# Searching key tiles 2 to 6 in the first part of a streaming encoder layer, with sixteen of twenty-six rounds on ScalarE

## What is computed

```python
h = rmsnorm(x, g_pre)
u_a, gate_a, q, k, v, qi, ki, wi, gate_b = split(h @ w_in)
# index scores: 8 heads of width 32
dots  = einsum('bqhd,bkd->bqhk', qi, ki)
score = einsum('bqh,bqhk->bqk', wi, relu(dots)) * INDEX_SCALE
score = where(key_chunk <= query_chunk, score, -inf)     # chunks of 64
_, sel = top_k(score, 256)
# softmax attention of 8 query heads over the selected keys only, with a bias by distance,
# times silu(gate_b); the pool branch times silu(gate_a); concat -> w_out -> rmsnorm -> + x
```

## Time and profile before

| | |
|---|---|
| runs (median of 3) | 1626.82 us (1625.3 to 1630.24) |
| the profiled execution | 1626.64 us, its span 1624.8 us |
| TensorE busy | 1494.8 us (92%) |
| VectorE busy | 1141.5 us (70%) |
| ScalarE busy | 889.3 us (55%) |
| GpSimd busy | 455.9 us (28%) |
| granted TensorE clock, mean | 0.98 |

### The profile page before, as it was taken

The page is one execution under the profiler, slowest core; times in us unless marked ns, Lnnn a source line. Parts: engine busy times, 40 slices in busy tenths (PEclk is TensorE's granted clock), DMA queues, the critical chain, the costliest instruction groups (busy, mean ns, idle before and its releaser), DMA issues.

```text
span 1624.8 us, 17105 instructions
## 1 busy us (share of the span) xinstructions
PE 1494.8 (92%) x4935; PEld 841.4 (52%) x4935; DVE 1141.5 (70%) x2742; ACT 889.3 (55%) x1684; POOL 455.9 (28%) x387
## 2 busy tenths in 40 slices
PE   7999899989999999988788888989998989899996
PEld 4555555555554887756334444444444444455552
DVE  5412577769899566765388898999999889874412
ACT  3112333333334445553898888988997877533331
POOL 0111211121110322311444444344423333232341
PEclk9999999999999999988899999999999999999999
DMA  9322222231111211136822222331130211203011
GB/s 368 68 60 47 78 55 64 56 102 48 60 50 51 67 42 37 49 113 181 240 60 90 84 74 57 96 99 61 43 105 27 70 39 45 72 16 105 33 40 45
DMA packets 93158, 125.69 MB, mean 77 GB/s; under 512 B 17309, under 2 KB 64221, under 8 KB 92682
## 3 DMA queue, kind: packets, MB, share of 16 engines
q1 hardware_dynamic: 91834, 120.68, 23.8%
q10 hardware_dynamic: 1232, 3.93, 2.2%
HBM read 75.93 MB, written 47.61 MB: 76 GB/s over the span
## 4 chain that ended last, share of the span: by engine, by line
PE 25%; DVE 15%; issue 7%; ACT 5%; DMA 0%; POOL 0%; POOLq 0%; DVEq 0%; SPq 0%; ACTq 0%
PE wide L1791 9%; PE wide L1776 8%; DVE above L345 5%; DVE max_junk L1852 4%; PE bank L1751 2%; PE bank L1752 2%; PE bank L1753 2%; ACT act_junk L1667 2%; PE bank L1724 2%; DVE above L377 1%; ACT E L1704 1%; PE wide L1724 1%; DVE root L296 1%; ACT sq L1689 1%; DVE reach L378 1%
## 5 line engine op out<-in xcount | busy, mean ns | idle before, releaser
L938 PE MATMUL bank<-hT,home 128*128 128x512 f32 (+2 forms) x1280 | 485.9, 515 | 5.1 <-DVE sga L1153 2.4
L1627 POOL TENSOR_TENSOR E<-E,home 128x512 f32<-128x512 f32 (+1 forms) x174 | 226.5, 1305 | 460.0 <-ACT E L1704 460.0
L938 PEld LDWEIGHTS bank<-hT,home 128*128 128x128 f32 x1280 | 235.1, 191 | 164.6 <-issue 143.3
L1776 PE MATMUL wide<-E,home 128*128 128x512 f32 x544 | 281.9, 600 | 0.7 <-POOL E L1627 0.7
L1704 ACT ACTIVATE E<-bank 128x512 f32<-128x512 f32 (+1 forms) x290 | 165.4, 570 | 206.1 <-PE bank L1753 186.9
L914 ACT ACTIVATE relu<-wide 128x1024 f32<-128x1024 f32 (+7 forms) x192 | 154.0, 802 | 214.3 <-PE wide L956 154.2
L1192 DVE SCALAR_TENSOR_TENSOR S<-relu,wi,S 128x1024 f32<-128x1024 f32 (+7 forms) x168 | 173.8, 1035 | 101.6 <-ACT relu L914 94.2
L1852 DVE CUSTOM_DVE_ANT_0 max_junk<-bank,mask 128x512 bf16<-128x512 f32 (+3 forms) x235 | 138.3, 606 | 85.4 <-PE bank L1724 71.9
L1791 PE MATMUL wide<-home 128*128 128x512 f32 x272 | 140.9, 609 | 26.3 <-ACT osb L1693 26.0
L1667 ACT ACTIVATE act_junk<-S,minus_cand 128x1152 uint8<-128x1152 f32 (+5 forms) x105 | 155.5, 1481 | 1.6
L956 PE MATMUL wide<-kiT,qiT 96*128 96x512 f32 (+3 forms) x304 | 137.9, 522 | 7.2 <-ACT relu L914 7.2
(11 more groups left out here) (215 smaller groups left out, 2225.5 us busy)
## 6 DMA issues: line engine op xcount, KB each, us to landing
xs<-x_prompt SPq DMA_DIRECT2D x16, 512.0 KB, 4.2
home<-w_in SPq DMA_DIRECT2D x16, 512.0 KB, 13.2
xr<-x_prompt SPq DMA_DIRECT2D x16, 512.0 KB, 4.1
y_prompt<-osb SPq DMA_DIRECT2D x16, 512.0 KB, 2.8
first_q<-q_high_scratch SPq DMA_DIRECT2D x24, 256.0 KB, 4.6
s_scratch<-S SPq DMA_DIRECT2D x11, 512.0 KB, 2.7
gb<-gb_scratch SPq DMA_DIRECT2D x17, 256.0 KB, 4.9
home<-ma_scratch SPq DMA_DIRECT2D x17, 256.0 KB, 5.0
```

Source lines behind the costliest of these rows:

```text
L938: mm = pe.matmul(out, stationary(c), moving(c), start=(c == 0), stop=(c == DC - 1))
L1627: pool.tensor_tensor(E[:, k % 4, :, 0:n], E[:, k % 4, :, 0:n], EB[:, kv * GRP:(kv + 1) * GRP, off:off + n], ALU.mult)\
L1776: pe.matmul(wide[0][:, kv * 512:kv * 512 + GRP * n].rearrange("p (j n) -> p j n", j=GRP), values[:, kt, kv:kv + 2, :].rearrange("p a d -> ...
```

## The change

Tile 6 joins `EARLY`, and `FIRST` becomes 7. An early tile's search is now one scaling pass on ScalarE (SN), sixteen single rounds on ScalarE (SK), ten single rounds on VectorE (SP) and the four parts of the choice one by one (SC). `seek` is called by `project`: it takes portions until their planned costs pass the room (3.4 us a projection, 1.87 in the blocks of two and three tiles, 3.4 for every TM), and lays them evenly between the pieces of the projection. A load or a store of the search is placed only where no portion is taken. ScalarE's scratch row changes its type to 8 bits. VectorE gets one more wait on its own chain before it overwrites unseen scores. The code that builds the second part's order is the same and works on ten tiles instead of eleven.

```diff
+SEARCH_ROOM = 3.4
...
-EARLY = range(TOPK // P, 6)
-SEARCH_PIECES = [(r, min(r + 4, ALL_ROUNDS)) for r in range(0, ALL_ROUNDS, 4)]
+EARLY = range(TOPK // P, 7)
+CHOICES = 4
...
+def early_search(t):
+    n = key_tiles(t)
+    return ([(("SN", t), 0.14 * n)] + [(("SK", t, r), 0.143 * n + 0.78) for r in range(ZOOM_AT)]
+            + [(("SP", t, r), 0.155 * n + 0.45) for r in range(ZOOM_AT, ALL_ROUNDS)]
+            + [(("SC", t, part), 0.3 * n + 0.3) for part in range(CHOICES)])
...
-    def project(step, left):
+    def project(step, left, room=0.0):
         k = -(-len(pending) // left) if left > 0 else 0
         pieces = [pending.pop(0) for _ in range(min(k, len(pending), 2 * DC if step[0] == "TM" else DC))]
         aside = [short.pop(0) for _ in range(min(len(short), 2))]
         for i, piece in enumerate(aside):
             pieces.insert((i + 1) * (len(pieces) + len(aside) - i) // (len(aside) + 1) if pieces else i, piece)
         inside[step] = pieces
-        steps.extend(pieces)
+        seek(list(pieces), room)
         steps.append(step)
 
-    def seek():
-
-        if seeking:
-            steps.append(seeking.pop(0))
-            if steps[-1][0] == "SM" and seeking:
-                steps.append(seeking.pop(0))
+    def seek(pieces, room):
+
+        taken = []
+        while seeking and room > 0 and seeking[0][0][0] not in ("SL", "SM"):
+            item, cost = seeking.pop(0)
+            taken.append(item)
+            room -= cost
+        if not taken:
+            while seeking and seeking[0][0][0] in ("SL", "SM"):
+                steps.append(seeking.pop(0)[0])
+        marks = sorted([((i + 0.5) / len(pieces), 0, x) for i, x in enumerate(pieces)]
+                       + [((i + 0.4) / len(taken), 1, x) for i, x in enumerate(taken)], key=lambda m: m[:2])
+        steps.extend(x for *_, x in marks)
...
+            room = (SEARCH_ROOM if nt == 4 else 0.55 * SEARCH_ROOM)
             if t:
-                seek()
-                project(("TM", t), 1 + sum(taking))
+                project(("TM", t), 1 + sum(taking), SEARCH_ROOM)
                 pool_part()
             cached = 0 <= t - 4 < PAST // P
             for j, step in enumerate(mine):
                 scale(2)
-                if step[0] != "Q":
-                    seek()
-                project(step, sum(taking[j:]) if taking[j] else 0)
+                project(step, sum(taking[j:]) if taking[j] else 0, room)
...
             if t - 1 in EARLY:
-                seeking.append(("SL", t - 1))
-                seeking += [("SP", t - 1, *piece) for piece in SEARCH_PIECES]
-                seeking.append(("SM", t - 1))
-                if len(seeking) == len(SEARCH_PIECES) + 2:
-                    steps.append(seeking.pop(0))
+                seeking.append((("SL", t - 1), 0))
+                seeking.extend(early_search(t - 1))
+                seeking.append((("SM", t - 1), 0))
     spread(100)
     pool_part()
     settle()
-    while seeking:
-        seek()
+    steps.extend(item for item, _ in seeking)
     return steps, inside
...
-        junk = sb(st, "junk", [P, D], BF16)
+        junk = sb(st, "junk", [P, D], U8)
...
+                    elif s[0] == "SN":
+                        t = s[1]
+                        row = Se[:, 0:key_tiles(t) * P]
+                        act.wait_ge(Se_in, 16 * (t - EARLY[0] + 1))
+                        act.activation(row, row, ACT.Copy, scale=unit[:, t:t + 1]).then_inc(early_halved, 1)
+                        halvings = halved_by(t, 0, 0)
+                    elif s[0] == "SK":
+                        _, t, r = s
+                        w = key_tiles(t) * P
+                        act.wait_ge(early_halved, halved_by(t, r, 0))
+                        act.wait_ge(ss_done, norms)
+                        if r == 0:
+                            act.activation(junk[:, 0:w], Se[:, 0:w], ACT.Sign, accum_out=tally[:]).then_inc(early_halved, 1)
+                        else:
+                            act.activation(junk[:, 0:w], Se[:, 0:w], ACT.Sign, bias=minus_cand[:], accum_out=tally[:])\
+                               .then_inc(early_halved, 1)
+                        if t == EARLY[0] and r == 0:
+                            act.wait_ge(early_enough, len(EARLY))
+                        act.wait_ge(early_halved, halved_by(t, r, 1))
+                        act.activation(side[:], tally[:], ACT.Sign, bias=enough[:, t - EARLY[0]:t - EARLY[0] + 1])\
+                           .then_inc(early_halved, 1)
+                        act.wait_ge(early_halved, halved_by(t, r, 2))
+                        if r == 0:
+                            if t > EARLY[0]:
+                                act.wait_ge(early_taken, t - EARLY[0])
+                            act.activation(minus_cand[:], side[:], ACT.Copy, scale=-half_width(r)).then_inc(early_halved, 1)
+                        else:
+                            act.activation(minus_cand[:], side[:], ACT.Identity, scale=-half_width(r), bias=minus_cand[:])\
+                               .then_inc(early_halved, 1)
+                        halvings = halved_by(t, r + 1, 0)
...
                     elif s[0] == "SP":
-                        _, t, first, last = s
+                        _, t, r = s
                         w = key_tiles(t) * P
-                        if first == 0:
-                            dve.wait_ge(Se_in, 16 * (t - EARLY[0] + 1))
-                            n = normalise(dve, dve_chain, n, B, [Se[:, 0:w]], [unit[:, t:t + 1]])
-                        n = halve(dve, dve_chain, n, B, [Se[:, 0:w]], first, last)
-                    elif s[0] == "SM":
-                        t = s[1]
+                        if r == ZOOM_AT:
+                            dve.wait_ge(early_halved, HALVED * (t - EARLY[0] + 1))
+                            dve.tensor_scalar(B.cand[:], minus_cand[:], -1.0, None, ALU.mult).then_inc(early_taken, 1)
+                            dve.wait_ge(early_taken, t - EARLY[0] + 1)
+                        n = halve(dve, dve_chain, n, B, [Se[:, 0:w]], r, r + 1)
+                    elif s[0] == "SC":
+                        _, t, part = s
                         w = key_tiles(t) * P
-                        if t > EARLY[0]:
+                        if t > EARLY[0] and part == 0:
                             dve.wait_ge(m_out, 16 * (t - EARLY[0]))
-                        for part in range(CHOICES):
-                            n = choose(dve, dve_chain, n, B, Se[:, 0:w], part)
-                        dve.tensor_scalar(B.reach[:, 0:w], B.reach[:, 0:w], MASKED, None, ALU.mult)\
-                           .then_inc(m_ready, 1)
+                        n = choose(dve, dve_chain, n, B, Se[:, 0:w], part)
+                        if part == CHOICES - 1:
+                            dve.tensor_scalar(B.reach[:, 0:w], B.reach[:, 0:w], MASKED, None, ALU.mult)\
+                               .then_inc(m_ready, 1)
...
+                        dve.wait_ge(dve_chain, n)
                         blind, x = (slice(0, CHUNK), b - CHUNK) if t < NPT else (slice(0, P), PAST + DEC)
```

More of the change, by code:

```diff
@@ L312, in __init__ @@
             sb(st, f"search{keys}_{i}", [P, tiles], F32) for i in range(6))
+HALVED = 1 + 3 * ZOOM_AT
 def half_width(r):
     return 2.0 ** -r
-def normalise(dve, done, n, B, scores, units):
-    for s, unit in zip(scores, units):
-        dve.tensor_scalar(s, s, unit, None, ALU.mult).then_inc(done, 1)
-    dve.memset(B.cand[:, 0:len(scores)], 0.0).then_inc(done, 1)
-    return n + len(scores) + 1
 def recentre(dve, done, n, B, scores):
@@ L356, in halve @@
     return n
-CHOICES = 4
 def choose(dve, done, n, B, s, part):
@@ L455, in phase1 @@
         Se = sb(st, "Se", [P, key_tiles(EARLY[-1]) * P], F32)
+        tally, side = (sb(st, f"early_{i}", [P, 1], F32) for i in range(2))
+        minus_cand = sb(st, "early_minus_cand", [P, 1], F32)
+        enough = sb(st, "early_enough", [P, len(EARLY)], F32)
         rows = sb(st, "rows", [HIST, 2, DPOOL], F32)
@@ L723, in _ @@
                                        pattern=[[-1, P]], channel_multiplier=1).then_inc(ident_done, 1)
+                for t in EARLY:
+                    pool.memset(enough[:, t - EARLY[0]:t - EARLY[0] + 1], key_tiles(t) * P - 2.0 * TOPK + 1.5)\
+                        .then_inc(early_enough, 1)
                 chain = 0
@@ L797, in turn, with halved_by @@
                         act.wait_ge(fa_free, k)
+                def halved_by(t, r, part):
+                    return HALVED * (t - EARLY[0]) + 1 + 3 * r + part
                 low_parts = {fa[x] for x in steps if x[0] == "Q"}
+                norms = halvings = 0
                 for s in steps:
@@ L812, in _ @@
                             act.wait_ge(ss_done, i)
+                        if halvings:
+                            act.wait_ge(early_halved, halvings)
+                        norms = i + 1
```

(1 more changed line is left out.)

1 line of the change is left out of this document (added).

## The result

| | before | after |
|---|---|---|
| median of 8 runs each, us | 1627.89 (1622.36 to 1630.56) | 1635.28 (1632.57 to 1638.93) |
| profiled execution, us (span) | 1626.64 (1624.8) | 1632.57 (1630.8) |
| first part, to the first logit matmul | 762.8 | 787.4 |
| second part, from there to the end of the span | 862.0 | 843.4 |

The last two rows are of the profiled executions. The ratio of after to before is 1.0051, 95% interval 1.0036 to 1.0066. The forecast was 1621 us and faster; 1635.28 lies in the range of 1605 to 1639. The second part gave back 18.6 us (forecast 18). The first part lost 24.6 (forecast 13).

A forecast was written before the change was run, and what follows sets the result against it. TensorE's matmuls bound the first part; in the second it also waits behind search passes on ScalarE and VectorE. Terms -18 + 9 + 2 + 4 - 3 + 1, and -1 for clock, make -6: 1621 us, range 1605 to 1639.

The forecast's parts named there:

- Second part, -18: Second part: with tile 6's search gone from ScalarE and VectorE, TensorE waits less; 18 us gained.
- ScalarE by tile 6, +9: First part, fourth block: tile 6 gives ScalarE 49.2 us of work in 40; 9 us lost.
- VectorE's sum for tile 5: First part, 514 to 568 us: VectorE's work with tile 5's rounds, 50.6 us in 54, fits; nothing lost.
- VectorE by tile 6, +4: First part, 612 to 666 us: VectorE 6.4 us over, relu buffers absorb some 2; 4 us lost.
- Full stretches of tiles 4 and 5 (+2): First part: ScalarE's work fits but its queues are nearly full, with waits now and then; 2 us lost.
- relief (-3): First part: VectorE no longer blocks the relu buffers for four rounds at once; 3 us gained.
- wait and load (+1): First part: VectorE's wait before overwriting unseen scores, and ScalarE perhaps waiting for tile 6's scores; 1 us lost.
- early tiles (0): First part: tiles before 4 are shorter and ScalarE's free time covers them; nothing lost.
- The clock, -1: Second part: less clock lost behind TensorE's stalls, which get fewer; 1 us gained.
- The slower one: Rival, 0.29: query transposes wait behind ScalarE's rounds and the clock falls; first part +26, second -14, 1639 us.
- No change: Rival, 0.25: the second part gives 12 to 15 us, the first loses 13 or so; 1626 us.
- Much faster: Rival, part of the 0.46 for faster: ScalarE's excess caught up next stretch; first part loses 5, second gives 24; 1608 us.

The follow-up runs named there:

- e2: The changed kernel with ScalarE's passes for tile 6 in the first part counting over 16 of its 896 scores; one run, 1627.97 us.
- e1: The changed kernel with the ten VectorE rounds of tile 5 in the first part counting over 16 of 768 scores; one run, 1628.74 us.
- e10: A control: the kernel before, with only the eight bias stores issued two per tile in the first four tiles; 1626.51 us, ratio 0.9991.
- e3: The change with tiles 2 to 5 only, tile 6 back in the second part; 1633.77 us, ratio 1.0034.
- e4: The kernel before with tile 6 added to its early tiles, in portions of four rounds, all on VectorE; 1637.72 us, ratio 1.0072.
- e9: e5 with tile 7 (1024 keys) searched in the first part as well; 1608.34 us, ratio 0.9874.
- e5: The change's search passes placed by a budget per engine, VectorE's cut for norms, with a second score row over the bias rows; 1610.21 us, ratio 0.9895.
- e6: e5 with bigger budgets, room 3.6 and 3.0 us a projection for 3.0 and 2.6; 1611.21 us, ratio 0.9904.
- e8: e5 with tile 6 held back to the place the change gave it, its rounds as close as there; 1620.47 us, ratio 0.9948.

## Why the prediction was wrong, step by step

- **Second part, -18: held**, at -18.6. Its sign for the waits was half wrong. The maxima's fell by 10.9 us, 27%; the output bank's rose by 1.5. TensorE's idle time fell from 88.6 to 77.2 us, 11.4, and the other 7.2 are busy time (773.4 to 766.2) for the same 2372 recorded matmuls. So the size came out right for a reason that I gave only in part.
- **ScalarE by tile 6, +9: the number came out, 8.4 us, but by luck.** My price of 30.0 us adds up instructions that overlap: the counting pass at 598.45 us lasts 1.04 us, and its readout starts 0.93 us after it. Between the marks ScalarE's busy time rose by 25.0 us (20.1 to 45.1); with the short gaps between its instructions it is some 4 us over the 43.9 there, and not 9. The sign that I had named, over 0.93 busy between 573 and 625 us, failed: 39.8 of 52 us, 0.77. The loss came from what stands in front of the evacuations that TensorE needs: waits of 4.6 and 1.8 us and 2.0 us of longer matmuls. e2 took 6.2 us of the step away by making the passes short.
- **The failed step** is VectorE's sum for tile 5, from 514 to 568 us: "50.6 in 54, nothing". It cost 10.9 us, 7.2 of them idle and 3.7 longer matmuls; e1 gave 9.1 back. On average the load just fits: VectorE's 46.5 us of work between the marks fill the 48.0 that the stretch had taken, with some 1 us over. In its order it does not. Between the two gate products VectorE was full already for 11.4 us, two norms among it, and four rounds made that 16.7, with TensorE waiting for the second of them. I had found in the very same sum that an average over the whole kernel hides a stretch, and then averaged over one that still hides the queue. With 10.9 in the place of nothing the sum would have come out at +5 and not at -6, and the sign with it.
- **VectorE by tile 6, +4: mis-sized**, 8.8 us. The 24.3 us of work were 20.5 on the engine (55.3 to 75.8), which the 82.3 us between the marks would hold, but they stand in the first part of it: VectorE works 64.0 of the 66.5 us from 632.0 to 698.5. I had let the two relu buffers absorb 2 of 6.4 us; 6.0 us were lost even in e2, where the second step leaves little behind.
- **Full stretches of tiles 4 and 5 (+2), relief (-3), wait and load (+1), early tiles (0)**: the second block lost 2.6 us, where I had nothing, but e10, with the order of before but for its stores, loses 1.6 there, so no price of tiles 2 and 3 is shown. The third block gained 5.8, where +2 and -3 stood; e1, e2 and e3, with the same order there, gained 5.1 to 5.4, while e4 and e10 lost 0.6 and 1.7 with the old one. The relief was real and larger than I allowed.
- **The clock, -1: too small, and only half of it.** In the second part the busy time fell by 7.2 us, as said. In the first part I had no loss at all. TensorE was idle 41.4 us in the first part before and 56.5 after, 15.1 more. The other 9.5 of the 24.6 us are busy time, 721.4 to 730.9 for the same 2563 or 2564 recorded matmuls, with a mean granted clock of 0.98 and 0.97. After the wait of 4.1 us that ends at 561.6 the granted clock was 0.66 from 560 to 570, and after the wait of 4.6 that ends at 600.8 it was 0.83 from 600 to 610, partly at the lower of the two levels, where the kernel before had 1.00. The Trainium skill ("TensorE: Matmul & The Clock Gate", section on HAM oscillation) says that idle gaps let the gate fall back and that work then starts cold; by that rule a stall is paid twice, and these rows agree. I charged that only to the rival. The balance of a whole part is a weaker witness: e3 has the first step with its 3.7 us of longer matmuls, and its first part is busy 721.1 us all the same, as before.

**The rivals.** The slower one (0.29, 1639 us) came closest: the first part ended past 785, as it says, and lost 24.6 for its 26; its second part gave 14, not 18.6. Its own mechanism, the transposes behind ScalarE's rounds with the clock after them, is there (3.4 to 10.1 us of waits for the transposes' evacuation), but it is one of three steps and not the first; what made the sign was VectorE at tile 5, which no rival had. "No change" asked for a second part that gives only 12 to 15. "Much faster" had ScalarE's excess caught up in the next stretch; but the marks after each step show no return, since the next stretch is full of TensorE work.

**Open.** Why the second tile moved (7, in e9) brought 1.8 us in the second part when the first brought 14.9 was not tried. TensorE's waits for the output bank fell there (22.0 us for e5's 27.3) and those for the maxima rose (31.5 for 29.0), so another order of the same waits is part of it. Nor was it tried why the second part took 843.4 us in the change and in e4 but 847 in e1, e2, e5, e6 and e8. Differences of a single execution of that size are inside the spread of one kernel's runs (1622.4 to 1630.6 us). Which part of e5's edit carries its gain (the second row, a budget for each engine, or the cut for norms) was not parted either; e8 shows only that the gain falls from 16 to 8 us when tile 6 stands late and close. And no run varied how many rounds may stand in front of a bank-freeing job, so no length of queue that is still harmless can be given.

## What to carry to other kernels

When work moves under a bound engine, do not stop at the load of each helper engine over a stage: here it all but fitted, 46.5 us in 48.0, and cost 10.9. Find the short jobs that free a bank, and add up what stands in the queue from one of them to the next, with single long jobs (two norms of 2.7 us) put in by name; where the engine does not wait between two of them already, each new portion goes straight onto the bound engine's wait. Take the price of a portion from the distance of starts, not from the sum of durations. Expect a long stall to show twice, as idle time and as longer matmuls (7.2 and 3.7 us here). And if the sum is near zero, ask first whether the same work can be put elsewhere: the change's own search, spread by each engine's load, turned +0.5% into about -1%.

## What the hardware showed that I had not expected

- Stalls of 4.1 and 4.6 us were followed by granted clocks of 0.66 and 0.83, each over a stretch of 10 us; in all 9.5 us of the loss appear as longer matmuls, not as waits.
- 24.9 us of busy time taken from ScalarE left the waits for its output copies where they were (26.0 and 27.5 us in 22 waits): between these two kernels they did not follow that engine's load.
- Durations of neighbours on ScalarE overlap, so their sum is not the time that they take: sixteen rounds and a scaling pass add up to 30.0 us, and the engine was busy 25.0 us longer.
- VectorE's running count over 768 keys took 1.75 us in the kernel before and 2.28 in the kernel after, on the same shape and types. No run says why.
- The wait that a profile names can be two steps from its cause: relu L963 for TensorE, and the score product on VectorE for relu (5.32 us).
